# Two transformer blocks in one program: first loads regrouped by queue and order, scaling ahead of squares, position biases spread as short copies

## The reference

```python
for layer in range(DEPTH):          # first block, DEPTH = 2
    u = rms_norm(x, norm_mix_g[layer])
    proj = jnp.einsum('bsd,de->bse', u, w_in[layer])
    (a_in, bq, bk, bv, cq, ck, cv, co, cgate, dq, dk, dv, gates) = split_cols(proj)
    y_a = fourier_mix(a_in)
    y_b = gqa_branch(...); y_c = mlstm_branch(...); y_d = diff_branch(..., rel_bias, layer + 1)
    x = x + merged @ w_out[layer]
    x = x + conv_ffn(rms_norm(x, norm_ffn_g[layer]), ...)
```

## Time and profile before

| | us |
|---|---|
| median of 3 runs | 3438.64 (3433.9 to 3439.54) |
| the profiled execution | 3442.09 |
| its span | 3440.8 |
| PE busy | 3348.7 (97%) |
| DVE, ACT, POOL busy | 1520.3, 1394.3, 1409.3 |

### The profile page before, as it was taken

How to read it: one execution, slowest core, us unless ns; L and a number is a source line. 1 busy time by engine, 2 the same in 40 slices (tenths; PEclk the granted TensorE clock), 3 DMA queues, 4 the chain that set the end, 5 groups by cost and what they waited for, 6 DMA issues and landing times.

```text
span 3440.8 us, 39040 instructions
## 1 busy us (share of the span) xinstructions
PE 3348.7 (97%) x14332; PEld 2559.9 (74%) x14332; DVE 1520.3 (44%) x2803; ACT 1394.3 (41%) x2610; POOL 1409.3 (41%) x1052
## 2 busy tenths in 40 slices
PE   7999999999999999999999999998999999899999
PEld 4667776787888766777688888864788887478887
DVE  4543556444435454456634464456322134632222
ACT  2443335533323354343544333446433235643322
POOL 1323332345545322333244555541355543235544
PEclk8999999999999999999999999999999999999999
DMA  4122121223322211211123322210232222013222
GB/s 153 62 80 71 62 68 61 74 95 110 105 98 94 78 62 62 68 62 68 60 88 120 109 98 95 92 62 25 73 110 96 98 92 68 25 65 108 98 96 101
DMA packets 154882, 284.69 MB, mean 83 GB/s; under 512 B 17984, under 2 KB 20321, under 8 KB 154692
## 3 DMA queue, kind: packets, MB, share of 16 engines
q1 hardware_dynamic: 153204, 279.81, 24.6%
q10 hardware_dynamic: 1488, 2.39, 0.3%
HBM read 276.76 MB, written 5.37 MB: 82 GB/s over the span
## 4 chain that ended last, share of the span: by engine, by line
PE 92%; DVE 4%; ACT 3%; DMA 1%; issue 1%; POOL 0%; ACTq 0%; SPq 0%; DVEq 0%; POOLq 0%
PE bank L543 26%; PE bank L545 26%; PE bank L544 26%; PE bank L601 3%; PE bank L610 2%; PE bank L777 1%; PE bank L791 1%; PE bank L789 1%; PE bank L575 1%; PE bank L912 1%; PE bank L734 1%; PE bank L658 1%; PE bank L838 1%; DMA raw<-in_units 1%; PE bank L904 1%
## 5 line engine op out<-in xcount | busy, mean ns | idle before, releaser
L2114 POOL TENSOR_TENSOR wl<-raw,wh 128x512 fp32r<-128x512 f32 x1012 | 1378.4, 1369 | 2016.4 <-ACT wh L981 1993.4
L543 PE MATMUL bank<-Uh,wh 128*128 128x512 f32 x2720 | 1125.3, 414 | 14.9 <-DVE Ul L1428 11.3
L545 PE MATMUL bank<-Uh,wl 128*128 128x512 f32 x2720 | 1068.6, 393 | 0.0
L981 ACT ACTIVATE wh<-raw 128x512 fp32r<-128x512 f32 x1012 | 625.3, 626 | 1089.9 <-PE bank L545 1068.6
L544 PE MATMUL bank<-Ul,wh 128*128 128x512 f32 x2720 | 1066.7, 392 | 0.0
L543 PEld LDWEIGHTS bank<-Uh,wh 128*128 128x128 f32 x2720 | 515.1, 189 | 174.5 <-issue 53.0
L544 PEld LDWEIGHTS bank<-Ul,wh 128*128 128x128 f32 x2720 | 515.7, 190 | 121.9 <-issue 18.4
L545 PEld LDWEIGHTS bank<-Uh,wl 128*128 128x128 f32 x2720 | 514.4, 189 | 110.7
L1417 DVE TENSOR_TENSOR work<-bank,rs 128x512 f32<-128x512 f32 x308 | 212.7, 691 | 783.3 <-PE bank L545 745.4
L543 PE MATMUL bank<-Hh,wh 128*128 128x512 f32 x1258 | 505.4, 402 | 4.5 <-DVE small L1692 1.9
L545 PE MATMUL bank<-Hh,wl 128*128 128x512 f32 x1258 | 490.9, 390 | 0.0
(11 more groups left out here) (232 smaller groups left out, 2766.3 us busy)
## 6 DMA issues: line engine op xcount, KB each, us to landing
raw<-in_units SPq DMA_DIRECT2D x1012, 256.0 KB, 2.6
xT<-in_xT SPq DMA_DIRECT2D x8, 256.0 KB, 11.0
scratch<-work SPq DMA_DIRECT2D x1, 2048.0 KB, 14.1
out<-xT SPq DMA_DIRECT2D x8, 256.0 KB, 2.8
table<-scratch SPq DMA_DIRECT2D x4, 448.0 KB, 5.3
scratch<-table SPq DMA_DIRECT2D x1, 1152.0 KB, 5.2
work<-in_dft SPq DMA_DIRECT2D x2, 512.0 KB
work<-in_counts SPq DMA_DIRECT2D x2, 512.0 KB, 5.6
```

What stands on the lines that cost most here:

```text
L543: nc.tensor.matmul(out, H, xh, start=k == 0, stop=False)
L545: mm = nc.tensor.matmul(out, L, xh, start=False, stop=k == x.kt - 1)
L981: nc.scalar.activation(g.wh[:, a:a + PK * P], g.raw[:, a:a + PK * P], ACT.Copy).then_inc(s_hi, 1)
L2114: nc.gpsimd.tensor_tensor(g.wl[:, a:a + PK * P], g.raw[:, a:a + PK * P], g.wh[:, a:a + PK * P].bitcast(F32), ALU.subtract).then_inc(g.s_lo, 1)
```

## The change

- The parts of x and the first pieces are issued in another order by SP (piece 0, x 0 to 4, piece 1, x 5 to 7, pieces 2 and 3), and all loads of `first_loads` but the first vectors move from ACT's queue to SP's: the small ones that the spreads and the mean need (`second_loads`) behind piece 3, the others (`third_loads`) behind the transforms and piece 6.
- ACT scales the eight parts of x first, splits fewer pieces between them, and squares after that. DVE subtracts all eight first and sums after that.
- PE finishes products a0 and a1, then does the spreads, then the mean.
- A spread gives 32 copies of each of 4 heads' rows (3 matmuls in all, with 16 copies of each of 6 heads for the second table). SP writes 4 by 32 by 1024 and 6 by 16 by 384 values to HBM. The skewed read takes 32 or 16 partitions at a time: 16 and 48 DMAs instead of 4 and 6, one behind each weight piece.
- Waits are adapted (`select` 64 for 48 and one instruction group earlier on ACT, `table1` 16 loads for 4, `table2` split in two waits), and DVE no longer waits for `scratch1` ahead of the gates.

```diff
@@ -612,29 +612,24 @@
 
     def layer1(i):
         l = i
+        finish_of(i, "a", 0)
+        finish_of(i, "a", 1)
         if i == 0:
             pe.wait_ge(g.landed["spread1"], 32)
-            for h in range(4):
-                for a in range(2):
-                    b = 2 + (2 * h + a) % 4
-                    take(b, s_dve, "V", "spread1", h, a)
-                    nc.tensor.matmul(bank[b][:, :], g.merged[0:NB, 2 * S + h * P:2 * S + (h + 1) * P],
-                                     g.merged[0:NB, a * S:(a + 1) * S], start=True, stop=True).then_inc(
-                                         s_pe, T("spread1", h, a))
-        finish_of(i, "a", 0)
-        if i == 0:
+            pe.wait_ge(g.landed["spread2"], 32)
+            m = g.merged
+            by_head = m[0:NB, 2 * S:2 * S + P]
+            for a in range(2):
+                nc.tensor.matmul(bank[2 + a][:, :], by_head, m[0:NB, a * S:(a + 1) * S], start=True, stop=True).then_inc(
+                    s_pe, T("spread", a))
+            by_head = m[0:NB, 4 * S:4 * S + 96]
+            nc.tensor.matmul(bank[4][0:96, 0:L2], by_head, m[0:NB, 3 * S:3 * S + L2], start=True, stop=True).then_inc(
+                s_pe, T("spread", 2))
+            for a in range(3):
+                take(2 + a, s_dve, "V", "spread", a)
             pe.wait_ge(g.landed["const"], 32)
         norm_mean(i, "mix")
         beat(i, "F", 0)
-        if i == 0:
-            pe.wait_ge(g.landed["spread2"], 32)
-            for h in range(6):
-                b = 2 + h % 4
-                take(b, s_dve, "V", "spread2", h)
-                nc.tensor.matmul(bank[b][:, 0:L2], g.merged[0:NB, 4 * S + h * P:4 * S + (h + 1) * P],
-                                 g.merged[0:NB, 3 * S:3 * S + L2], start=True, stop=True).then_inc(
-                                     s_pe, T("spread2", h))
-        finish_of(i, "a", 1)
         beat(i, "F", 1)
         pe.wait_ge(g.landed["dft"], 16 * 5 * (l + 1))
 
...
@@ -1170,14 +1167,18 @@
     def layer1(i):
         where["products"] = 0
         if i == 0:
-            split_weights(-RING + 2)
+            split_weights(-RING + 1)
             act.wait_ge(g.landed["vec0"], VEC_LANDED[0])
             for k in range(KD):
                 act.wait_ge(g.s_x[k], 16)
                 nc.scalar.activation(tile(g.Uh, k), tile(g.xT, k), ACT.Copy, scale=g.v1(0, "mix", k)).then_inc(
                     s_act, C("Uh", 0, "mix", k))
+                if k % 4 == 3:
+                    split_weights(-RING + 2 + k // 4)
+            for k in range(KD):
                 model_tile(0, "mix", k, None, w(25 + k % 2))
-                split_weights(-RING + 2 + k // 2)
+                if k == 2:
+                    split_weights(0)
             act.wait_ge(g.landed["const"], 32)
...
@@ -1557,8 +1559,6 @@
         gi, gf, *_ = g.gate_tiles()
         finished(i, x)
         dve.wait_ge(s_act, at("C", "rs", i, "mix"))
-        if i == 0:
-            dve.wait_ge(g.landed["scratch1"], 16)
...
@@ -1867,27 +1867,21 @@
         where["products"] = 0
         gq = small[:, 40:41]
         if i == 0:
-            rows = g.work[:, 17 * S:25 * S]
-            for h in range(4):
-                for a in range(2):
-                    b = 2 + (2 * h + a) % 4
-                    dve.wait_ge(s_pe, at("T", "spread1", h, a))
-                    nc.vector.tensor_copy(rows[:, h * L1 + a * S:h * L1 + (a + 1) * S], bank[b][:, :]).then_inc(
-                        s_dve, V("spread1", h, a))
             dve.wait_ge(g.landed["vec0"], VEC_LANDED[0])
             for k in range(KD):
                 dve.wait_ge(g.s_x[k], 16)
-                model_tile(0, "mix", k, g.v1(0, "mix", k), w(25 + k % 2))
+                lower(tile(g.Ul, k), tile(g.xT, k), tile(g.Uh, k), ("C", "Uh", 0, "mix", k), "U", 0, "mix", k,
+                      scale=g.v1(0, "mix", k))
+            for k in range(KD):
+                model_tile(0, "mix", k, None, w(25 + k % 2))
+            for a, rows, cols in ((0, P, S), (1, P, S), (2, 96, L2)):
+                dve.wait_ge(s_pe, at("T", "spread", a))
+                nc.vector.tensor_copy(g.table[0:rows, a * S:a * S + cols], bank[2 + a][0:rows, 0:cols]).then_inc(
+                    s_dve, V("spread", a))
         else:
             dve.wait_ge(g.landed[f"vec{i % 2}"], VEC_LANDED[i])
         nc.vector.tensor_scalar(gq, g.v1(i, "q"), HQ ** -0.5, None, ALU.mult).then_inc(s_dve, V())
         beat(i, "F", 0)
-        if i == 0:
-            for h in range(6):
-                b = 2 + h % 4
-                dve.wait_ge(s_pe, at("T", "spread2", h))
-                nc.vector.tensor_copy(g.table[:, h * L2:(h + 1) * L2], bank[b][:, 0:L2]).then_inc(
-                    s_dve, V("spread2", h))
         beat(i, "F", 1)
 
         def features(p):
...
@@ -2174,30 +2170,42 @@
         nc.sync.dma_start(w(11), dft[:, 5 * S:6 * S]).then_inc(landed["dft"], 16)
         nc.sync.dma_start(w(12)[:, 0:2 * P], dft[:, 8 * S:8 * S + 2 * P]).then_inc(landed["dft"], 16)
 
-    def skewed(scratch, h, L, n):
-
-        return bass.AP(tensor=scratch.tensor, offset=h * P * L + P - 1, ap=[[L - 1, P], [1, n]])
+    def skewed(scratch, h, L, n, first, rows):
+
+        return bass.AP(tensor=scratch.tensor, offset=h * P * L + P - 1 - first, ap=[[L - 1, rows], [1, n]])
+
+    def copies(scratch, a, heads, rows, L, name):
+
+        sp.wait_ge(g.s_dve, at("V", "spread", a))
+        src = g.table[0:heads * rows, (a // 2) * 2 * S:(a // 2) * 2 * S + L]
+        nc.sync.dma_start(scratch[:, 0:rows, :], src).then_inc(landed[name], 16)
+
+    def tables(scratch, heads, rows, L, pitch, n, name):
+
+        for h in range(heads):
+            for first in range(0, P, rows):
+                weights(where["piece"] + 1)
+                nc.sync.dma_start(g.table[first:first + rows, h * pitch:h * pitch + n],
+                                  skewed(scratch, h, L, n, first, rows)).then_inc(landed[name], 16)
 
     weights(1)
-    x_tile(0)
-    weights(2)
-    for k in range(1, KD):
+    for k in range(KD):
         x_tile(k)
+        if k == 4:
+            weights(2)
     weights(4)
+    second_loads(g)
+    weights(6)
     transforms()
-    sp.wait_ge(g.s_dve, at("V", "spread1", 3, 1))
-    nc.sync.dma_start(A["scratch1"].rearrange("h p l -> p h l"),
-                      g.work[:, 17 * S:25 * S].rearrange("p (h l) -> p h l", h=4)).then_inc(landed["scratch1"], 16)
+    weights(7)
+    third_loads(g)
     weights_before(0, "a", 3)
-    sp.wait_ge(g.s_dve, at("V", "spread2", 5))
-    nc.sync.dma_start(A["scratch2"].rearrange("h p l -> p h l"),
-                      g.table[:, 0:6 * L2].rearrange("p (h l) -> p h l", h=6)).then_inc(landed["scratch2"], 16)
+    copies(A["scratch1"], 1, 4, 32, L1, "scratch1")
+    copies(A["scratch2"], 2, 6, 16, L2, "scratch2")
     weights_before(0, "cq", 0)
     sp.wait_ge(landed["scratch1"], 16)
     sp.wait_ge(landed["scratch2"], 16)
-    for h in range(4):
-        nc.sync.dma_start(g.table[:, h * E1:(h + 1) * E1], skewed(A["scratch1"], h, L1, E1)).then_inc(
-            landed["table1"], 16)
+    tables(A["scratch1"], 4, 32, L1, E1, E1, "table1")
     for i in range(2 * DEPTH - 1):
         weights_before(i, "f1a" if i < DEPTH else "f2a", 2)
         sp.wait_ge(g.s_used, g.product(i, "out1" if i < DEPTH else "out2", KD - 1).done)
...
-                nc.sync.dma_start(g.table[:, h * 2 * P:(h + 1) * 2 * P], skewed(A["scratch2"], h, L2, 2 * P)).then_inc(
-                    landed["table2"], 16)
+            tables(A["scratch2"], 6, 16, L2, 2 * P, 2 * P, "table2")
     weights(len(g.pieces))
     i = 2 * DEPTH - 1
...
 
-def first_loads(g):
-
-    nc, A, landed = g.nc, g.A, g.landed
-    m, (sel, n), (eps, _) = g.merged, CONST["select"], CONST["eps"]
-    vectors_of(g, nc.scalar, 0)
-    nc.scalar.dma_start(m[0:NB, 0:L1], A["onehot1"]).then_inc(landed["spread1"], 16)
-    nc.scalar.dma_start(m[0:NB, 2 * S:3 * S], A["rb1"]).then_inc(landed["spread1"], 16)
-    nc.scalar.dma_start(g.const[:, 0:sel], A["const"][:, 0:sel]).then_inc(landed["const"], 16)
-    nc.scalar.dma_start(g.const[:, eps - n:NCONST - n], A["const"][:, eps:NCONST]).then_inc(landed["const"], 16)
-    nc.scalar.dma_start(m[0:NB, 3 * S:3 * S + L2], A["onehot2"]).then_inc(landed["spread2"], 16)
-    nc.scalar.dma_start(m[0:NB, 4 * S:4 * S + 6 * P], A["rb2"]).then_inc(landed["spread2"], 16)
+def second_loads(g):
+
+    nc, A, landed, m = g.nc, g.A, g.landed, g.merged
+    sel, (eps, _), n = CONST["select"][0], CONST["eps"], CONST["select"][1]
+    nc.sync.dma_start(g.const[:, 0:2 * P], A["const"][:, 0:2 * P]).then_inc(landed["const"], 16)
+    nc.sync.dma_start(g.const[:, eps - n:NCONST - n], A["const"][:, eps:NCONST]).then_inc(landed["const"], 16)
+    nc.sync.dma_start(m[0:NB, 0:L1], A["onehot1"]).then_inc(landed["spread1"], 16)
+    nc.sync.dma_start(m[0:NB, 2 * S:2 * S + P].rearrange("b (h p) -> b h p", p=32),
```

(14 more changed lines are left out.)

20 lines of the change are left out of this document (14 added, 6 removed).

## The result

| kernel | median us | range | ratio to before, 95% interval |
|---|---|---|---|
| before | 3439.01 | 3433.9 to 3439.54 | |
| changed | 3413.15 | 3409.69 to 3416.05 | 0.9926 (0.9914 to 0.9938) |

The change gains 25.9 us; forecast were 23.3 (3415.3), with a range of 3404 to 3425. The profiled execution of the changed kernel took 3410.6 (span 3409.3), 2.6 less than its median; that of before took 3442.1, 3.1 more than its own. So the two traces differ by 31.5, and 5.6 of that is luck of the two executions.

What follows compares the result with a forecast made beforehand. TensorE, busy 97% of the span, bounds the kernel, so only its waits or droppable work count. First layer gains 29.8 us, second loses 6.5: 23.3 off the 3438.6 median gives 3415.3 us, range 3404 to 3425.

Steps and rivals of the forecast that it cites:

- the mark: Start of the first Fourier features in the first layer, forecast to move from 61.1 to 29.3 us.
- Arrival: Start of the first layer: the last part of x lands at 11 us instead of 19.9.
- rival B: First layer: x is no faster and lands at 19.9 as before; 3422 us; chance 10%.
- The first two products: First layer: the first product ends near 14.5 us, the second at 20; VectorE's sums are hidden.
- The bare stretch: Mean to eviction 2.51 us and fold 3.56, uncovered ahead of the first layer's features, ending at 28.5.
- The transforms: First layer: the last transform loads, behind the 127-row load, land at 28 to 30 us; taken 29.3.
- Second layer: Mean behind the second product leaves PE resting ahead of the features: 4.7 us plus 1.8 of clock, 6.5 lost.
- Hidden: Scratch writes, loads moved behind piece 6 and the 64 table loads cost nothing on the path.
- Rival A: First layer: writes of the spread copies hold weight pieces back, third features wait 5 to 7 us; 3421; chance 11%.
- Rival C: Both layers: fold without POOL beside it and no fall of the clock; 3409 us; chance 12%.
- D: Each of 64 table loads holds the next weight piece 0.43 us and PE waits: 27.6 us, 3442.9; chance 3%.
- E: Start of the kernel: nothing gained, because PE's work and not its waits set the start; 3435 us; chance 2%.

Runs made afterwards that it cites:

- kernel 5: Changed kernel with all small loads and tables (2.1 MB) issued by ACT ahead of its first instruction again; 3419.04 us.
- kernel 6: Changed kernel with a square of each part of x right behind its scaling, and the fourth piece's split behind the last square; 3417.58 us.
- kernel 9: kernel 4 with ACT splitting pieces 4, 5 and 6 right behind its last square, ahead of the mean's Ln; 3397.02 us.
- kernel 2: Changed kernel with the 127-row transform load made as two loads of 112 and 15 rows; 3409.45 us.
- kernel 8: Changed kernel with six throwaway matmuls between the mean and the first features, in both layers; 3413.90 us.
- kernel 1: Changed kernel with the mean between the two products again, in the second layer alone; 3409.07 us.
- kernel 3: Changed kernel with the two scratch writes of the spread copies moved behind the weight pieces up to those ahead of the first table load; 3411.18 us.
- kernel 7: Changed kernel with each of the 64 skewed table loads made as two loads of half the rows; 3417.23 us.
- kernel 4: Changed kernel with the edits of kernel 1, kernel 2 and kernel 3, and the first layer's spreads behind the mean; 3399.06 us.

## Why the prediction was right, and where it was not

- *What bounds the kernel, and the mark.* Right. 22.1 of the 23.3 us that the sum speaks of are found at the two places that it names.
- *What in the change made the 31.0 us.* The prediction has 22 us of spreads "dropped in plain sight", but its own rows don't let them be counted in full. In before the last copy of the first spread was done at 21.9 (row below), but SyncE could not issue the fifth piece before 25.63, behind the one-row load that blocked until 23.7, and PE stood 8.09 us for what hung on that piece. With the first spread alone made short, the piece would still have been issued only then, and most of the 14 us would have gone into a longer rest there. This is read from the rows, no run shows it. The second spread's 8 us had no rest behind them. So the new order of pieces and transforms has a share in what looks like the first spread's gain. No run takes the spreads, or this order, back by itself: kernels 5 and 6 give 5.5 and 6.5 us for their two parts of the change, and how the rest of the 31.0 divides stays open.

```profile
21.18 0.69 DVE L1875 COPY work<-bank 128x512 f32<-128x512 f32 x1 [1.02 <-PE bank L621]
```

- *Arrival.* The last part of x lands at 11.2 (said: 11), the engines move 344 GB/s from 2 to 10 us (said: 333). So the condition of rival B, x at 19.9 as before, didn't come. But the reason behind the gain was weighed wrong. I led with the shared engines and gave ACT's queue half a sentence. Kernel 5 puts 2.1 MB back beside x, and ACT's issues bind, not the landing: x at 15.2 cost nothing there. What x at 19.9 would have cost by itself wasn't tried.
- *The first two products.* Said: a1 ends at 20; it ends at 21.1. Steps 4 to 7 weren't bound by piece 1 alone: four subtractions for x took 4.22 us on VectorE while POOL worked beside it, and PE waited 0.61 for one at 14.82. Kernel 6 shows the same engine as the bound. It is the same slip twice: I priced ACT's part, left VectorE's subtractions without a price and called its sums hidden.
- *Spreads.* 2.56 us, said 2.4. The working has a slip: three fp32 matmuls leave 6 records, not 10, and only with 6, the last two of them shorter, do 0.44 us each come to 2.4.
- *The bare stretch.* Mean to eviction 2.61 (said 2.51), to the fold's end another 3.51 (said 3.56). POOL beside the fold is what makes its two subtractions 1.08 and 1.48 us; kernel 9 shows 0.41 and 0.42 without it. The second layer's rows were the right ones to price the first layer's.
- *The transforms.* 30.05, said 28 to 30, taken 29.3. They and the fold end 0.2 us apart, so repairing one of them alone gives nothing at the mark (kernel 2). The load of 127 rows was named as the cause, and kernel 2 shows it.
- *Clock.* 2.3 us, said 2.0; kernel 8 shows that the rest is its cause, 2.2.
- *First layer.* 28.7 gained, said 29.8: 0.8 is the transforms' landing (30.05 for 29.3), 0.3 the clock. Without the transforms it would hardly be better, since a1's 1.1 us put the fold at 29.85.
- *Second layer.* 6.6 lost, by both comparisons (before with changed, changed with kernel 1); said 6.5. Of the 6.6, 5.2 are the wait ahead of the features and 1.4 the clock (changed with kernel 1: the features 4.8 and the tokens 6.2 apart, each with the 0.4 of before); said were 4.7 and 1.8. That the sum fits to 0.1 is in part luck.
- *Hidden.* Right in the outcome. Rival A's margin was wrong: I counted 6 us of slack, and there were 0.17. The pieces were late for two causes that I had not added up: the 127-row load blocks SyncE's issues in the changed kernel too (5.36 us), and the issues of the two writes took another 5.5, of which 1.47 are left when the 127 rows are split (kernel 2). Each alone leaves slack (2.74 us in kernels 2 and 3).
- *Rival C* (both bare stretches cheap) didn't come, nor did D (kernel 7), nor E.
- *What the sum left out.* 25.9 - 22.1 = 3.8 us. Up to 2.3 of it can lie at 768, where PE's rest was 2.25 in this trace, 2.4 to 2.7 in five others and 3.3 in one, against 3.63 in the one trace of before; with one trace of before I can't tell whether this comes from the change. The rest is within the spread of the medians. So the forecast of 23.3 stands between the 22.1 found in the traces and the 25.9 of the medians, and the traces can't say which is nearer.

The version that the experiments point to is kernel 4, or 9 (which of the two is open): mean between the products in the second layer, the 127-row load split, copies late, spreads behind the mean.

## What to carry to other kernels

Of a gain at the start, ask which engine delivers the last operand there, and price that engine's own queue: here fourteen DMA issues on ACT cost more than the late bytes (kernel 5), and VectorE's sums bound, not ACT's squares (kernel 6). When lines are moved for one case, read what they do in the others; two lines outside a condition gave back 6.6 of the first layer's 28.7 us. A load with 127 rows that weight pieces follow in the same queue is better made as 112 and 15 (kernel 2).
